# A five-piece beginning of the first hidden stage, and two banks of values turned inside the last tile of the first attention's projection

## The reference

```python
def rms_norm(x, g):
    y = xf * lax.rsqrt(jnp.mean(xf * xf, axis=-1, keepdims=True) + EPS)
    return (y * g).astype(x.dtype)

def macaron_half(x, g, w_in, w_out):
    a, b = jnp.split(rms_norm(x, g) @ w_in, 2, axis=-1)
    return x + 0.5 * ((jax.nn.silu(a) * b) @ w_out)

def diff_layer(x, ...):
    x = macaron_half(x, p['g_ffn1'], p['w_ffn1_in'], p['w_ffn1_out'])   # D_FF = 2816
    hn = rms_norm(x, p['g_attn'])
    q, k, v, qm = jnp.split(hn @ p['w_in'], [768, 1536, 2304], axis=-1)
    q = rms_norm(q by head, p['g_q']); k = rms_norm(k by head, p['g_k'])
    # two softmaxes per head, their difference times v, memory attention beside it
    x = x + mix @ p['w_out']
    return macaron_half(x, p['g_ffn2'], ...), k, v
```

## Time and profile before

| | us |
|---|---|
| median of 3 runs | 1278.88 (1278.86 to 1279.47) |
| the profiled execution | 1280.21 |
| its span, first to last instruction | 1278.4 |
| PE busy in the span | 1265.4 |
| DVE busy, ACT busy, POOL busy | 741.6, 561.2, 174.8 |

### The profile page before, as it was taken

One profiled execution on the slowest core, in us unless ns is written; L12 is line 12 of the kernel. 1 busy time (PEld: TensorE's weight loads), 2 busy tenths in 40 slices (PEclk: granted clock), 3 DMA queues, 4 the chain that ended last, 5 costly groups with the idle time before them and its releaser, 6 DMA issues.

```text
span 1278.4 us, 22446 instructions
## 1 busy us (share of the span) xinstructions
PE 1265.4 (99%) x8784; PEld 1243.9 (97%) x8784; DVE 741.6 (58%) x1128; ACT 561.2 (44%) x827; POOL 174.8 (14%) x208
## 2 busy tenths in 40 slices
PE   9999999999999999999999999999999999999999
PEld 8999999999998999999999999999997899999999
DVE  7756574555677656554454675554446756656433
ACT  7534363353275533333343453433345763343322
POOL 0300020046143100000122000000124510000000
PEclk9999999999999999999999999999999999999999
DMA  8454445553203444444443533454451144343443
GB/s 279 163 160 150 161 139 174 195 188 132 100 34 130 164 151 145 160 163 139 151 164 123 196 133 138 157 164 160 135 187 34 55 144 159 137 164 131 135 140 128
DMA packets 39661, 187.45 MB, mean 147 GB/s; under 512 B 4369, under 2 KB 14353, under 8 KB 24497
## 3 DMA queue, kind: packets, MB, share of 16 engines
q1 hardware_dynamic: 38272, 183.38, 41.8%
q0 software_dynamic: 1184, 3.13, 1.1%
q10 hardware_dynamic: 144, 0.11, 0.0%
HBM read 179.70 MB, written 6.90 MB: 146 GB/s over the span
## 4 chain that ended last, share of the span: by engine, by line
PE 95%; DVE 2%; ACT 1%; issue 1%; DMA 1%; SPq 0%; ACTq 0%; DVEq 0%
PE bank L490 29%; PE bank L492 29%; PE bank L491 29%; PE bank L752 1%; PE bank L713 1%; PE bank L890 1%; PE bank L755 1%; PE bank L722 1%; DVE wlo L1526 1%; DMA raw<-in_w_ffn_in 1%; ACT whi L1120 0%; PE outs L516 0%; ACT ew L1281 0%; PE outs L518 0%; PE outs L500 0%
## 5 line engine op out<-in xcount | busy, mean ns | idle before, releaser
L490 PE MATMUL bank<-xhi,whi 128*128 128x320 f32 (+1 forms) x1760 | 545.8, 310 | 3.0 <-DVE wlo L1901 1.1
L492 PE MATMUL bank<-xhi,wlo 128*128 128x320 f32 (+1 forms) x1760 | 543.0, 309 | 0.0
L491 PE MATMUL bank<-xlo,whi 128*128 128x320 f32 (+1 forms) x1760 | 543.0, 309 | 0.0
L1526 DVE TENSOR_TENSOR wlo<-raw,whi 128x2048 fp32r<-128x2048 f32 (+1 forms) x177 | 364.1, 2057 | 230.2 <-ACT whi L1120 230.1
L1120 ACT ACTIVATE whi<-raw 128x2048 fp32r<-128x2048 f32 (+1 forms) x177 | 304.1, 1718 | 242.3 <-PE bank L492 237.9
L490 PEld LDWEIGHTS bank<-xhi,whi 128*128 128x128 f32 x1760 | 330.5, 188 | 6.2 <-issue 3.4
L491 PEld LDWEIGHTS bank<-xlo,whi 128*128 128x128 f32 x1760 | 330.6, 188 | 0.5
L492 PEld LDWEIGHTS bank<-xhi,wlo 128*128 128x128 f32 x1760 | 330.5, 188 | 0.0
L490 PE MATMUL bank<-hhi,whi 128*128 128x320 f32 x704 | 219.0, 311 | 0.0
L492 PE MATMUL bank<-hhi,wlo 128*128 128x320 f32 x704 | 217.5, 309 | 0.0
L491 PE MATMUL bank<-hlo,whi 128*128 128x320 f32 x704 | 217.5, 309 | 0.0
(11 more groups left out here) (233 smaller groups left out, 1041.5 us busy)
## 6 DMA issues: line engine op xcount, KB each, us to landing
raw<-in_w_ffn_in SPq DMA_DIRECT2D x86, 1024.0 KB, 4.8
raw<-in_w_ffn_out SPq DMA_DIRECT2D x64, 704.0 KB, 4.2
raw<-in_w_in_a SPq DMA_DIRECT2D x10, 1024.0 KB, 4.8
raw<-in_w_out SPq DMA_DIRECT2D x8, 1024.0 KB, 4.9
raw<-in_w_kv SPq DMA_DIRECT2D x6, 1024.0 KB, 4.8
raw<-in_w_mkv SPq DMA_DIRECT2D x4, 1024.0 KB, 4.7
raw<-in_w_in_b SPq DMA_DIRECT2D x4, 1024.0 KB, 4.7
raw<-in_w_ffn_in SPq DMA_DIRECT2D x8, 256.0 KB, 7.2
```

Source lines behind the costliest of these rows:

```text
L490: mm(acc, wh, mhi(ks[q]), start=start and q == 0, stop=False)
L491: mm(acc, wh, mlo(ks[q]), start=False, stop=False)
L492: last = mm(acc, wl, mhi(ks[q]), start=False, stop=stop and q == nk - 1)
L1526: tt(wlo[slot][:, 0:size], raw[slot][:, 0:size], f32(whi[slot][:, 0:size]), ALU.subtract).then_inc(lo_ready[slot], 1)
```

## The change

In the beginning:

- x and the first two blocks come in five pieces of 1, 1, 2, 2 and 2 terms (`START`), each piece of x followed by the same terms of both blocks. The first piece of the second block is issued by ACT, right after `early`. ACT and DVE split each piece of both slots before they go on, and PE multiplies it for slot 0 and then slot 1.
- The squares and all their sums come after the last piece. PE's `row_norm` moves from the middle of slot 1 of the first pair to behind the first product of the second pair, and ACT's and DVE's behind the splits of both blocks of the second pair (the third block in halves, the fourth whole).
- The third block is loaded in two halves, each as soon as its half of slot 0 has been used up by the splits; the fourth and the memory follow.
- The first two products of the second pair go into banks 4 and 5, so that they need not wait for gate 0 and gate 1. The product of the bias table therefore goes into `HS`, and after the fourth product of that pair.
- 15 matmuls on ones in place of 19. `settle` on ACT waits for `early` in place of the constants, and POOL's loads of the constants wait for the second half of the third block.
- x and the memory lie in the chip's memory by partitions, so that a piece of x is one row of 1280 or 2560 bytes for each partition, and the memory one of 8192.

In the projection `pa`: slot 2 is turned inside the last tile's product before its term 4, slot 3 before its term 6. DVE's copy of slot 3 is put before its reading of the last tile.

The diff, cut to its core:

```diff
+START = [(0, 1), (1, 2), (2, 4), (4, 6), (6, 8)]
+LAST = len(START) - 1
...
-            x_v = a["xT"].rearrange("(k p) r -> p k r", p=P)
-            for q in range(4):
-                sp.dma_start(x[:, 2 * q:2 * q + 2], x_v[:, 2 * q:2 * q + 2]).then_inc(d_x[q], 16)
-                sp.dma_start(raw[0][:, 512 * q:512 * (q + 1)], weights["in0"][0][:, 512 * q:512 * (q + 1)]
-                             ).then_inc(d_piece[q] if q < 3 else landed[0], 16)
...
+            for q, (k0, k1) in enumerate(START):
+                own = slice(256 * k0, 256 * k1)
+                sp.dma_start(x[:, k0:k1], x_v[:, k0:k1]).then_inc(d_x[q], 16)
+                sp.dma_start(raw[0][:, own], weights["in0"][0][:, own]
+                             ).then_inc(d_piece[q] if q < LAST else landed[0], 16)
+                if q:
+                    sp.dma_start(raw[1][:, own], weights["in0"][1][:, own]
+                                 ).then_inc(d_piece1[q] if q < LAST else landed[1], 16)
+            sp.wait_ge(piece_lo, 3)
+            sp.dma_start(raw[0][:, 0:BLK // 2], weights["in0"][2][:, 0:BLK // 2]).then_inc(d_third, 16)
+            sp.wait_ge(lo_ready[0], 1)
+            sp.dma_start(raw[0][:, BLK // 2:BLK], weights["in0"][2][:, BLK // 2:BLK]).then_inc(landed[0], 16)
+            sp.wait_ge(lo_ready[1], 1)
+            sp.dma_start(raw[1][:], weights["in0"][3]).then_inc(landed[1], 16)
+            sp.dma_start(memt[:], a["memT"]).then_inc(d_mem, 16)
...
+                    for q, (k0, k1) in enumerate(START):
+                        pe.wait_ge(xn_lo, k1)
+                        for slot, some in ((0, piece_lo), (1, piece1_lo)):
...
+                        spare = halves and j < 2
+                        if not spare:
+                            wait_acc(t0 + 4 * i + j)
...
-                        product(banks[j][:, 0:R], slot, col, 256, range(KD), KD,
+                        product(banks[4 + j if spare else j][:, 0:R], slot, col, 256, range(KD), KD,
...
-                    body(1, False, lambda j: stats() if j == 1 else None, halves=True)
+                    body(1, False, lambda j: row_norm(stage, R) if j == 0 else stats() if j == 3 else None, halves=True)
...
-            for _ in range(19):
+            for _ in range(15):
...
-                mm(banks[4][0:H_A, 0:NREL + 1], table[:], hot[:], start=True, stop=True).then_inc(trel_ready, 1)
+                mm(HS[0:H_A, 0:NREL + 1], table[:], hot[:], start=True, stop=True).then_inc(trel_ready, 1)
...
+            def within_pa(k):
+                if k == 4:
+                    turn_slot(AUX0["pa_v"] + 2, vT, [(v, 2 * P, 64, v * P) for v in range(4)])
+                if k == 6:
+                    turn_slot(AUX0["pa_v"] + 3, vT, [(4 + v, c * P, P, (2 * c + v) * P) for c in range(2) for v in range(2)])
...
             act.dma_start(early[:], a["early"]).then_inc(d_early, 16)
+            act.dma_start(raw[1][:, 0:256], weights["in0"][1][:, 0:256]).then_inc(d_piece1[0], 16)
...
+            for k in range(KD):
+                nc.scalar.activation(sq8[:, k, :], x[:, k, :], ACT.Square).then_inc(sq_ready, 1)
+            act.wait_ge(d_third, 16)
+            act.wait_ge(first_half, 1)
+            nc.scalar.activation(whi[0][:, 0:BLK // 2], raw[0][:, 0:BLK // 2], ACT.Copy).then_inc(third_hi, 1)
             act.wait_ge(landed[0], 16 * (PAIR0["in0"] + 1) + 16)
             act.wait_ge(acc_ready, TILE0["in0"] + 2)
-            nc.scalar.activation(whi[0][:, 0:BLK // 2], raw[0][:, 0:BLK // 2], ACT.Copy).then_inc(third_hi, 1)
+            nc.scalar.activation(whi[0][:, BLK // 2:BLK], raw[0][:, BLK // 2:BLK], ACT.Copy).then_inc(hi_ready[0], 1)
+            split_hi(1, PAIR0["in0"] + 1, BLK, acc_ready, TILE0["in0"] + 4)
             row_norm("in0", R)
-            nc.scalar.activation(whi[0][:, BLK // 2:BLK], raw[0][:, BLK // 2:BLK], ACT.Copy).then_inc(hi_ready[0], 1)
...
-            pool.wait_ge(landed[1], 16)
+            pool.wait_ge(landed[0], 32)
```

More of the change, by code:

```diff
@@ L548, in turn_values, with projection @@
                 return f
-            def projection(stage, w, groups, tiles, xin=(xhi, xlo), norm_at=0, after=None, before=None):
+            def projection(stage, w, groups, tiles, xin=(xhi, xlo), norm_at=0, after=None, before=None, within=None):
                 n0, t0, x0 = PAIR0[stage], TILE0[stage], XN0[stage]
@@ L563, in each @@
                             pe.wait_ge(xn_lo, x0 + k + 1)
+                    if within and j == tiles - 1:
+                        each = within
                     if stage == "kv" and j == tiles - 1:
@@ L598, in first_pieces @@
                                                lambda k: xhi[:, k, :], lambda k: xlo[:, k, :], True, True,
-                                               part=(2 * q, 2 * q + 1))
-                                if q == 3:
+                                               part=range(k0, k1))
+                                if q == LAST:
                                     last.then_inc(acc_ready, 1)
+                            if slot == 0 and k1 == KD // 2:
+                                last.then_inc(first_half, 1)
                 def body(i, first, after=None, halves=False):
@@ L1403, in _ @@
                     input_hi(x[:, k, :], xhi[:, k, :], "ffn1_0", k)
-                act.wait_ge(d_piece[q] if q < 3 else landed[0], 16)
-                nc.scalar.activation(whi[0][:, 512 * q:512 * (q + 1)], raw[0][:, 512 * q:512 * (q + 1)], ACT.Copy
-                                     ).then_inc(piece_hi if q < 3 else hi_ready[0], 1)
-            def squares(tiles):
-                for k in tiles:
-                    nc.scalar.activation(sq8[:, k, :], x[:, k, :], ACT.Square).then_inc(sq_ready, 1)
@@ L1412, in piece1 @@
-            def piece1(q):
-                act.wait_ge(d_piece1[q] if q < 3 else landed[1], 16)
-                nc.scalar.activation(whi[1][:, 512 * q:512 * (q + 1)], raw[1][:, 512 * q:512 * (q + 1)], ACT.Copy
-                                     ).then_inc(piece1_hi if q < 3 else hi_ready[1], 1)
-            piece1(0)
-            squares(range(4))
-            piece1(1)
-            squares(range(4, KD))
-            piece1(2)
-            piece1(3)
+                act.wait_ge(d_piece[q] if q < LAST else landed[0], 16)
@@ L1640, in body @@
                 def body(i, size, at=None):
+                    spare = stage == "in0" and isinstance(i, int) and i == 1
                     for c in range(2):
                         dve.wait_ge(acc_ready, t0 + 4 * i + c + 1)
-                        tt(gate[:, c, :], banks[c][:, 0:R], r[:], ALU.mult).then_inc(acc_free, 1)
+                        tt(gate[:, c, :], banks[4 + c if spare else c][:, 0:R], r[:], ALU.mult).then_inc(acc_free, 1)
                         if at:
@@ L1663, in ffn_in @@
                     for i in range(3):
-                        body(i, BLK, third if stage == "in0" and i == 0 else None)
+                        body(i, BLK)
                         after(i)
```

116 lines of the change are left out of this document (56 added, 60 removed).

## The result

The changed kernel takes **1284.72 us** (median of five runs, 1284.32 to 1285.80), the kernel before 1279.13 on the same chip (1278.86 to 1279.47): ratio 1.0046, 95% interval 1.0033 to 1.0058. It is 5.6 us slower. The forecast was 2.0 slower, and its range ended at 1283.4.

A forecast was written before the change was run, and what follows sets the result against it. PE was taken as the bound, busy 1265.4 of 1278.4 us. A third pair 2.6 us later less 0.6 at the end of `pa` gave +2.0 on the 1278.9 median: 1280.9 us, range 1279.0 to 1283.4.

The forecast's parts named there:

- rival 2: PE's idle time before the third pair brings its low clock back, losing 2.5 us: +4.5, 1283.4; chance 0.12.
- the term of the third pair: The third pair starts at 41.5 us against 38.91, 2.6 us later, with PE idle some 4.4 us.
- The first piece: At the start, smaller first loads let ACT begin at 4.85, DVE at 5.3 and PE at 5.8 us.
- The third piece and the end of the first pair: PE reaches the third piece at 11.0 us after pausing about 1.3, and ends the first pair at 21.5.
- What the beginning proper gains: The first pair ends at 21.5 us in place of 23.3: 1.8 us gained, up to 3.1.
- The chain from the norm to the third pair: From the row norm through both gates to the third pair takes 16.56 us in place of 19.68.
- The end of `pa`: Slots turned inside the last tile let unit 1's scores start 0.6 us sooner, bounds 0.3 to 0.9.
- Landings: Third block's second half and fourth block are split by 22.7 and 26.1 us, covered even if landing a microsecond later.
- Small ones: Later requests for the constants and the memory, and `settle`, stay hidden: all at 0.
- Rival 1: The third pair doesn't depend on gate 0, so PE goes on at 37.1: 1275.2 to 1276.5; chance 0.10.
- 4 (a norm before 24.3): The pieces at the start gain more, norm at 23.7 to 24.3 us: 1279.4 to 1280.0; chance 0.12.
- Rival 3: Last piece lands 1 to 2 us later, passing one to one into the third pair: +3.0 to +4.0; chance 0.13.

The follow-up runs named there:

- e9: The kernel before, unchanged, profiled a second time: 1279.17 us.
- e4: The changed kernel with all eight memory tiles' high and low parts moved from behind the first pair to behind the third: 1280.88 us, ratio 1.0013.
- e5: The changed kernel with the row norm ahead of the second pair on PE, and ahead of the fourth block's split on ACT and DVE: 1282.95 us, ratio 1.0022.
- e2: The kernel before with only slots 2 and 3 turned inside the last tile of `pa`: 1278.62 us, ratio 0.9997.
- e1: The changed kernel with the end of `pa` as before, so the changed beginning alone: 1285.91 us, ratio 1.0052.
- e3: The changed kernel with 25 useless matmuls on ones in PE's pause before the third pair: 1282.37 us, ratio 1.0024.
- e6: e5 with the memory's tiles split four behind the second pair and four behind the third: 1279.39 us, ratio 0.9997.
- e10: e2 with the memory's tiles split four, two and two behind the first, second and third pairs: 1277.80 us, ratio 0.9988.
- e8: The changed kernel with 12 matmuls on ones in PE's pause before the third pair: 1284.18 us (median of eight runs), ratio 1.0032.
- e7: e2 with the memory's tiles split four behind the second pair and four behind the third: 1278.82 us, ratio 0.9993.

## Why the prediction was wrong, step by step

Two steps failed. The sum put the low clock behind the pause at nothing (it was rival 2, at 0.12), and it costs 2.1 us or more. And the term of the third pair was set to 2.6 us, against a late row, and is 3.5. Even rival 2 as priced (1283.4) stays 1.3 us below the measured time.

**The first piece: right.** PE at 5.8 was forecast (5.2 to 6.6), 6.02 was measured; ACT 4.85 and 4.99, DVE 5.3 and 5.44.

**The third piece and the end of the first pair: nearly right.** Forecast 11.0 with a pause of 1.3 us, and 21.5; measured 10.44 with some 0.8, and 21.07.

**What the beginning proper gains: wrong by 0.6 us, because of the row it was set against.** The sum took 23.3 as the end of the first pair before. In e9 the norm stands 1.04 sooner than in the earlier trace rows, so the pair ends at about 22.25. The gain is 22.25 - 21.07 = 1.2 us, not 1.8, and some 0.5 of it is the norm that was moved out (the term of the prediction took 0.7 for it). The pause up to 10.31 in the earlier trace rows, on which the whole change seems to rest, was 1.3 us long in that execution and 0.6 in all in e9: ACT had the second quarter at 8.90 in the one and at 7.37 in the other. PE's start is 1.2 us sooner than in the earlier trace rows, but 0.7 sooner than in e9.

**The chain from the norm to the third pair: right.** Forecast 16.56, measured 41.36 - 24.73 = 16.63. Gate 0 at 28.19 (28.4 forecast), gate 0 of the second pair at 36.10 (36.3), the third pair at 41.36 (41.5), with PE idle 3.7 us (4.4) and a wait for up 0 beside it, as named. e4 and e5 show that both the memory's parts and the norm's place are in this chain. PE's own readiness was forecast 0.5 us too early (37.1; the pause begins at 37.6).

**How much later that is: the term that was mis-sized.** The sum had 41.5 - 38.91 = 2.6. The usual third pair of before is at 37.87 (e9) or 37.97 (e2), so it is 41.36 - 37.87 = 3.5. I saw that the profiled execution was 1.3 us above the median, and subtracted this from the end of the sum, as if the surplus were spread over the whole run. But 1.04 of it lay in the very row from which the term was taken. The new beginning doesn't share that surplus. It belonged to this term, and with it the sum would have given 1281.9.

**The low clock: the wrong choice between forecast and rival.** Rival 2 had the mechanism and its place, with a chance of 0.12; it came in all five runs of the changed kernel (mean clocks 0.997 and 0.999) and in all of e1. Its price was forecast as 2.5 us from the slow beginning; it is 2.1 by the trace (313.25 - 311.12 us from the third pair to the scores) and some 2.6 by the medians with and without the filled pause. I wrote that the rival decides only if the wait is about 4 us, forecast a wait of 4.4, and still gave it one chance in eight, on the ground that waits of up to 1.1 us had done nothing. (The longest waits of PE in that run are three of 1.3 us in the attention, for `pt` and `rs`, which the earlier trace rows leave out.) A wait three times as long was outside what these rows could speak for. The rival's evidence for the low level was the pace of the first matmuls, 0.28 us each. In that stretch the profile gives the granted clock as 1.00, so only the pace speaks for it there; behind the pause of the changed kernel both do. The Trainium skill, "TensorE: Matmul & The Clock Gate", section "Why this matters for your kernels", warns that a long idle gap between bursts brings the low clock back. The trace now agrees: 3.73 us idle, then 17 matmuls at 0.267 us with a granted clock of 0.50.

**The end of `pa`: right.** 0.6 was forecast (0.3 to 0.9). The trace gives 0.76 in e2 and the medians 0.8 and 0.9.

**Landings: right for PE, too early for the norm.** PE has no wait for the third or fourth block. But the low part of the fourth was forecast to end at 26.1, with a microsecond to spare for a late landing, ahead of the norm's step at 27.0. It ended at 27.2, after ACT had waited 1.43 us for the block, and the norm's step began right behind it at 27.15. That cost 0.1 us in the changed kernel (3.46 us from the norm to gate 0, 3.36 in e3), but 0.6 in e1. The reserve that the prediction saw there was not there.

**Small ones: right.** No wait for the constants or the memory shows.

**The sum again, from the runs:** 3.5 for the third pair, 2.1 for the low clock, less 0.5 for `pa` (311.66 in e9 against 311.12 in e3, from the third pair to the scores; 0.75 by e2), is 5.1. The scores of unit 1 come at 354.61 against 349.53 in e9, 5.1 later, and the spans differ by 5.1 (1282.5 and 1277.4): nothing is given back or lost behind that point. Of the 5.6 between the medians 0.2 more lie outside the span (1284.47 - 1282.5 against 1279.17 - 1277.4), and 0.3 between these two executions and their medians.

Rival 1 (the norm isn't the limit) and 4 (a norm before 24.3) did not occur. Rival 3 (later landings) did not occur at the last piece that it names; in e1 it did at the fourth block, with 0.56 us that went one to one into the third pair.

What stays open: whether the new beginning, with the norm early and the memory spread in smaller lots than in e6, would beat e10. By the traces it has 0.4 us to gain over e9 without its wait, and some 1.0 over e10, whose norm stands 0.55 later than that of e9; single traces are too few for either. It wasn't tried.

## What to carry to other kernels

A sooner start is worth nothing if it moves a small, long chain (here the norm and all that waits for it) behind more work of the bound engine: follow the chain to the next place where that engine waits, and price a pause of several microseconds on TensorE twice, once for its length and once for the slow matmuls behind it. When a forecast rests on one late row, look whether that row is usual: if the profiled execution is above the median, the surplus may sit exactly in the term that is being priced. Side work for DVE or ACT is best laid in small lots over several stages, and where the engines beside it are idle: 4, 2 and 2 tiles left no wait here, where 8 or 4 and 4 did.

## What the hardware showed that was not expected

- In the kernels whose trace has a pause of PE of 3.7 us (the changed kernel, five runs, and e1, four) or 3.1 us (e5, ten), every run has a mean clock below 1, and the three traces show the 1.2 GHz level. In the changed kernel it was granted from 39.2 us on, some 1.6 us after PE had fallen idle. In the profiled executions the pauses of 0.8 us in the beginning of the changed kernel and of 1.5 us in e4 brought nothing. With 1.8 us left, as in e8, it went both ways: two runs stayed at 1.000, six fell below.
- The low level doesn't last one length: some 6.8 us in the traces of the changed kernel (39.2 to 46.0) and of e1, 3.4 in that of e5 (39.4 to 42.8). In e5 the runs with a mean clock of 0.999 and of 0.997 differ by 1.1 us in their mean time (1282.3 and 1283.4); in the changed kernel the two kinds don't differ in time (1284.32 and 1285.80 against 1284.47 to 1285.24). Single runs show a lower mean clock in kernels whose trace has no long pause: one of ten in e2 took 1281.48 at 0.999, where the others took 1278.25 to 1279.20, one of ten in e6, one of nine in e3, and three of the 67 of the kernel before that ran beside the experiments. These runs have no trace.
- The landing of a quarter that stands in a full queue differs between executions. The same copy on ACT began at 8.90 us in one execution of the kernel before and at 7.37 in another, and at 7.82, 7.20 and 8.03 in e2, e7 and e10, which have the same beginning.
- DVE's eight `memlo` took 3.28 us with POOL idle and 5.19 us with POOL adding squares during 3.60 of them; four took 1.66 us with POOL idle in e10, and 3.28 and 3.61 in e6 beside the same kind of work (0.48 us for one against 0.96). No run changes POOL alone.
